# Moving a gating branch's input products between two stages of a two-block transformer kernel

## The chip, the cores and the metric

One core of a Trainium2 chip runs the whole kernel. The metric is the device time of one execution in microseconds, median of three runs. PE is TensorE (the matrix engine), DVE is VectorE, ACT is ScalarE, POOL is GpSimd, SP is SyncE, which here issues nearly all DMAs.

## What is computed

The reference has two blocks on 1024 tokens of width 1024. The first (two attention-like mixers) ends with y @ w_out and a layer norm. The second is the one that most of the change is in:

```python
mod = c @ ada_w[l] + ada_b[l]
shift1, scale1, gate1, shift2, scale2, gate2 = jnp.split(mod, 6, axis=-1)
h = _modulate(_rmsnorm(x, norm1_g[l]), shift1, scale1)
z = h @ w_in[l]
zu, zv, zr = jnp.split(z, [GMLP_WIDTH, 2 * GMLP_WIDTH], axis=-1)
y_a = _gmlp_mixer(zu, zv, ...)      # u = gelu(zu); v = layer_norm(gelu(zv)); u * (causal mix of v)
y_b = _rwkv7_mixer(zr, ...)         # r, k, v and low-rank xw, xa, xg; decay from tanh(xw) @ w2,
                                    # a from xa @ a2, gate from sigmoid(xg) @ g2; scan over tokens
y = jnp.concatenate([y_a, y_b], axis=-1) @ w_out[l]
x = x + gate1[:, None, :] * y
h = _modulate(_rmsnorm(x, norm2_g[l]), shift2, scale2)
y = _hier_moe(h, ...)
```

GMLP_WIDTH is 512, so zu and zv are 1024 columns of w_in; the RWKV part is 512 wide, 8 heads of 64, with low-rank widths 32 (xw), 32 (xa) and 96 (xg). All arithmetic named here is fp32. A 128x128 by 128x512 product in fp32 shows in the trace as two matmul instructions with a weight load each.

## The kernel before, in words

The kernel is a chain of stages with a barrier between them; in a stage each engine has its own instruction list, ordered by hand and tied by semaphores. PSUM's eight banks form two rings of four: ring A is emptied by ACT, ring D by DVE. A `take` of a bank waits until its use four takes ago is freed. Each engine does its list strictly in order.

**stage_out** (line 629, run for both layers of the first block) multiplies the 12 chunks of yT by w_out (six DMAs of 1 MB, `wo_landed`). For each of 8 token tiles it runs hf 0 over all 12 chunks, then hf 1 (L674); DVE adds the residual and normalises while PE is at the next tile; PE then turns the tile before (L615 for the second layer).

**stage_rwkv_pairs** (line 1399, 1669 to 2239 us) works on pairs of heads, c = 0 to 3, by a `script` that PE, ACT and DVE all follow. First `lora`: three groups of low-rank columns (32, 32 and 96 wide) against hT (L1494), 16 products each. Then the front of pair 0: `proj` r, k, v (L1504, weights in three buffers), `small` (L1515), `sums` (L1524, whose result feeds DVE's longest chain, with a reciprocal over 128x1024). Then per pair:

- `turn`: transposes of v, k, b, a (L1536) and the bonus (L1541);
- `A`: five products ab, X, ak, rb, rk (L1552), two ring D banks each; DVE masks ab (L1918, 1921, 1922) and X (L1924, L1925) before the others, and ak and rb need the banks of ab and X;
- `AV` (L1582), then five `level`s (L1562, L1569, L1573). After each level of pair c stands one step of the front of pair c + 1: proj r, k, v, small, sums. For the last pair there is none;
- `tail`: GH (L1593, four ring A banks, emptied by ACT, L1821), then MT (L1603), N (L1611, L1612), Q (L1619) on ring D (DVE, L1944 to L1951), then Yi (L1626, L1627) on ring A (ACT, L1824). SP stores MT, N, Q and Yi to DRAM (L1663, L1664).

ACT does the square roots and exponentials of `sums` (c + 1) (L1778 to L1783) before the GH copies of `tail` (c), since that is the script's order; DVE likewise does its `sums` before MT.

**stage_mix** (line 1976, 2239 to 2580 us) goes over token tiles t in a software pipeline. One iteration of PE is: u(t) (L2044), chain(2t) (L2059), v(t), chain(2t + 1), mix(t-1) (L2067), the RWKV rows(t-1) (L2079) with the gate product g (L2084), turn(t-2) (L2092), out(t-3) (L2100), the norm's turn(t-4) (L615), router(t-5) (L2108). The chain carries the state T from half tile to half tile: PE multiplies by mt, DVE adds n and scales (`step`, L2280, L2282), and the next chain product needs that. DVE's iteration is step(2t), gmlp_norm(t) (L2286 to L2295), step(2t + 1), gmlp_rows(t-1) (L2301, L2303), rwkv_rows(t-1) (L2311 to L2327), normalise(t-4), residual(t-3) (L2337, L2339). ACT's is gelu of u (L2229) and of v (L2232), square roots, copies of yT, and the norm's evacuation (L624). Weights for u and v (w_uv, 4 MB in two DMAs, L2145 and L2152) and the streams mt, n, qt, yi, v (256 KB each and tile) come on SP's queue, as do w_o (4 MB) and a store of zeros (7.7 MB) to the slots of the experts' stage.

## Time and profile before

| | us |
|---|---|
| median of 3 runs | 3325.42 (3325.37 to 3328.36) |
| the profiled execution | 3325.81 |
| its span in the profile | 3324.0 |
| PE busy | 2963.1 (89%) |
| DVE busy | 1724.7 (52%) |
| ACT busy | 1074.7 (32%) |
| POOL busy | 382.3 (12%) |

How to read what follows. Times are microseconds from the start of the span. Engines: PE is matmuls, PEld weight loads beside them. PEclk is the clock granted to TensorE as a share of 2.4 GHz; it has two levels, 1.0 and 0.5. A row of a timeline gives start, length, engine, line, operation, output <- inputs and how many instructions are merged in it (xN); in square brackets stands the idle time of that engine just before and what ended it. Matmuls are pipelined: each record is longer than the distance to the next.

### The profile page before, as it was taken

The numbers are of one execution on the slowest core, as the hardware profiler recorded it, in microseconds if no ns is written. First come the engines' busy times: TensorE is split into PE (matmuls) and PEld (weight loads), VectorE is DVE, ScalarE is ACT, GpSimd is POOL, SyncE is SP. The second block draws the span as 40 slices with busy tenths as digits, with TensorE's granted clock in tenths as the row PEclk, the third lists the DMA queues.
The fourth block names the chain that finished last, engine by engine and source line by source line (L and its number), as shares of the span: only waits on it lengthen the run. The fifth ranks groups of instructions, "written<-read, shape, count | busy, mean of one in ns | idle before, by whom it ended". The sixth has DMA issues, their size and how long they took to land. (4 is left out here: it accounts for less than half of the span.)

```text
span 3324.0 us, 44902 instructions
## 1 busy us (share of the span) xinstructions
PE 2963.1 (89%) x18196; PEld 2026.1 (61%) x18196; DVE 1724.7 (52%) x2719; ACT 1074.7 (32%) x1660; POOL 382.3 (12%) x318
## 2 busy tenths in 40 slices
PE   7999799898699999979987898877999499999990
PEld 6877544545577777754435666674555377777770
DVE  2223323454366665643316435533444699999984
ACT  2111100121355454441122212211223256565652
POOL 1322000000222222200021011010000000000001
PEclk9999899998899999989998897988999699999995
DMA  4111021741211121121011011028222699999985
GB/s 149 48 42 42 36 103 45 218 157 51 76 51 58 53 69 57 52 99 56 36 35 27 10 44 53 2 72 283 64 70 76 214 391 398 399 397 399 397 317 221
DMA packets 282433, 445.87 MB, mean 134 GB/s; under 512 B 14944, under 2 KB 148576, under 8 KB 282256
## 3 DMA queue, kind: packets, MB, share of 16 engines
q1 hardware_dynamic: 275200, 417.66, 35.7%
q0 software_dynamic: 7056, 25.69, 2.0%
q8 instruction: 130, 2.13, 0.3%
q14 instruction: 47, 0.39, 0.0%
HBM read 385.58 MB, written 57.74 MB: 133 GB/s over the span
## 5 line engine op out<-in xcount | busy, mean ns | idle before, releaser
L674 PE MATMUL psum<-wo,yT 128*128 128x512 f32 x768 | 337.7, 599 | 18.8 <-DMA wo<-in_w_out 18.7
L674 PEld LDWEIGHTS psum<-wo,yT 128*128 128x128 f32 x768 | 145.7, 192 | 201.4 <-issue 174.8
L906 PE MATMUL psum<-x_hi,w_hi 128*128 128x512 f32 x512 | 211.4, 413 | 29.4 <-POOL w_lo L1007 28.7
L1096 DVE TENSOR_TENSOR fox_pT_lo<-psum,fox_pT_hi 128x512 fp32r<-128x512 f32 (+2 forms) x192 | 107.1, 558 | 183.6 <-ACT fox_pT_hi L1035 174.4
L908 PE MATMUL psum<-x_hi,w_lo 128*128 128x512 f32 x512 | 201.5, 394 | 0.0
L907 PE MATMUL psum<-x_lo,w_hi 128*128 128x512 f32 x512 | 200.6, 392 | 0.0
L1504 PE MATMUL psum<-hT,wr 128*128 128x512 f32 x384 | 168.5, 597 | 0.0
L2699 ACT CAST hi_d<-land_d 128x2048 fp32r<-128x2048 f32 x66 | 122.7, 1908 | 140.5 <-PE psum L2571 140.5
L162 PE MATMUL psum<-x_hi,w_hi 128*128 128x512 f32 x384 | 151.9, 396 | 8.8 <-POOL w_lo L153 8.8
L2844 DVE TENSOR_TENSOR lo_d<-land_d,hi_d 128x2048 fp32r<-128x2048 f32 x66 | 148.3, 2288 | 21.5 <-ACT hi_d L2699 21.5
L1005 POOL CAST w_hi<-w_land 128x1024 fp32r<-128x1024 f32 x48 | 49.8, 1037 | 911.2 <-DMA w_land<-in_w_in 515.7
L163 PE MATMUL psum<-x_lo,w_hi 128*128 128x512 f32 x384 | 151.2, 394 | 0.0
L164 PE MATMUL psum<-x_hi,w_lo 128*128 128x512 f32 x384 | 150.7, 392 | 0.0
L2844 DVE TENSOR_TENSOR lo_g<-land_g,hi_g 128x2048 fp32r<-128x2048 f32 x66 | 150.6, 2283 | 0.0
L735 DVE SCALAR_TENSOR_TENSOR x_tile<-x_tile,psum 128x512 f32<-128x512 f32 x32 | 22.0, 688 | 244.0 <-PE psum L674 198.0
L1046 ACT ACTIVATE fox_p<-fox_p,fox_bias 128x256 f32<-128x256 f32 (+7 forms) x128 | 99.6, 778 | 120.2 <-DVE fox_bias L1082 116.3
L1504 PEld LDWEIGHTS psum<-hT,wr 128*128 128x128 f32 x384 | 72.8, 191 | 89.3 <-issue 88.7
L906 PEld LDWEIGHTS psum<-x_hi,w_hi 128*128 128x128 f32 x512 | 96.9, 189 | 48.3 <-POOL w_lo L1007 30.1
L2699 ACT CAST hi_g<-land_g 128x2048 fp32r<-128x2048 f32 x66 | 125.2, 1898 | 0.9 <-DMA land_g<-in_moe_w_gate 0.8
L2044 PE MATMUL psum<-w_uv,hT 128*128 128x512 f32 x256 | 117.0, 612 | 7.7 <-DMA rb<-in_router_expert_b 7.7
L2569 PE MATMUL psum<-hi_d,e_h_hi 128*128 128x512 f32 x264 | 116.5, 441 | 6.7 <-DVE e_h_lo L2861 6.7
L1079 DVE CUSTOM_DVE_ANT_0 fox_p<-psum,ncum 128x256 f32<-128x256 f32 (+7 forms) x128 | 97.0, 758 | 48.8 <-PE psum L925 40.2
(478 smaller groups left out, 6345.1 us busy)
## 6 DMA issues: line engine op xcount, KB each, us to landing
land_g<-in_moe_w_gate SPq DMA_DIRECT2D x66, 1024.0 KB, 8.0
land_u<-in_moe_w_up SPq DMA_DIRECT2D x66, 1024.0 KB, 9.1
land_d<-in_moe_w_down SPq DMA_DIRECT2D x66, 1024.0 KB, 9.6
ada<-in_ada_w SPq DMA_DIRECT2D x24, 1024.0 KB, 5.3
y_slots<-yb SPq DMA_DIRECT2D x33, 512.0 KB, 10.4
w<-in_w_in SPq DMA_DIRECT2D x24, 512.0 KB, 3.8
wo<-in_w_out SPq DMA_DIRECT2D x12, 1024.0 KB, 10.7
w_land<-in_w_in SPq DMA_DIRECT2D x24, 512.0 KB, 3.8
```

What stands on the lines that cost most here:

```text
L162: self.nc.tensor.matmul(bank[:], hi[:, d, :], E.x_hi[:, d, cols], start=(d == 0), stop=False)
L163: self.nc.tensor.matmul(bank[:], hi[:, d, :], E.x_lo[:, d, cols], start=False, stop=False)
L164: last = self.nc.tensor.matmul(bank[:], lo[:, d, :], E.x_hi[:, d, cols], start=False, stop=(d == ND - 1))
L674: last = nc.tensor.matmul(bank[:], E.yT[:, c, t * P:(t + 1) * P], wo[:, c, hf * HALF:(hf + 1) * HALF], start=(c == 0), stop=(c == NY - 1))
L906: nc.tensor.matmul(bank[:], hi[:, d, :], E.x_hi[:, d, cols], start=(d == 0), stop=False)
L907: nc.tensor.matmul(bank[:], hi[:, d, :], E.x_lo[:, d, cols], start=False, stop=False)
L908: last = nc.tensor.matmul(bank[:], lo[:, d, :], E.x_hi[:, d, cols], start=False, stop=(d == ND - 1))
L1504: last = nc.tensor.matmul(bank[:], w[m % NW][:, d, :], E.hT[:, d, hf * HALF:(hf + 1) * HALF], start=(d == 0), stop=(d == ND - 1))
L2044: last = nc.tensor.matmul(bank[:], E.hT[:, d, t * P:(t + 1) * P], w_uv[:, d, i * GW:(i + 1) * GW], start=(d == 0), stop=(d == ND - 1))
L2569: nc.tensor.matmul(bank, hi_t, hi_w, start=start, stop=False)
L2699: nc.scalar.copy(w_hi[x][:], land[x][:]).then_inc(hi_set[x], 1)
L2844: V.tensor_tensor(w_lo[x][:], land[x][:], w_hi[x][:].bitcast(F32), ALU.subtract).then_inc(lo_set[x], 1)
```

## The change

Five things change, and only these:

1. The 16 products for u and v of stage_mix (8 x 512 columns and 8 x 512) leave it. They are made in stage_rwkv_pairs as 32 units `("uv", q, t)`: for q = 0 to 3, a quarter (256) of the 1024 columns, and token tile t. A unit is 8 products, 16 instructions, of 256 columns on a ring A bank. `fill` says where they stand in the script: one after `small`(0), three before turn(0), one after X, ak, GH and N of each pair, one after levels 3 and 4 of pairs 1 to 3, one after rk and level 2 of pairs 1 and 2, two after Yi of pair 3. ACT copies each into one of two row buffers, SP stores it (128 KB) to `uv_dram`. `w_uv` now holds one quarter (1 MB); SP loads the next one when the last unit of a quarter is done.
2. stage_mix reads u and v as a stream of 512 KB tiles; gelu takes it from there. hT is freed before the stage, and w_uv is no longer loaded in it.
3. The low-rank groups xw and xa become one group of 64 columns (`xwa`), with w2 and a2 stacked in one tensor.
4. SP loads the projection weights for pair c + 1 one at a time in the script's order, where before it loaded three after the turn.
5. stage_out goes by chunk: for each chunk c both halves, with two banks taken first. (The line of w_o in stage_mix is only written differently: it was and is an fp32 product.)

The diff, cut to its core:

```diff
+                    banks = []
                     for hf in range(2):
                         bank, free = ringD.take(("y", t, hf))
                         wait(pe, ringD.free, free)
-                        for c in range(NY):
-                            if t == 0 and hf == 0 and c % 2 == 0:
-                                pe.wait_ge(wo_landed[c // 2], 16)
-                            last = nc.tensor.matmul(bank[:], E.yT[:, c, t * P:(t + 1) * P], wo[:, c, hf * HALF:(hf + 1) * HALF],
+                        banks.append(bank)
+                    for c in range(NY):
+                        if t == 0 and c % 2 == 0:
+                            pe.wait_ge(wo_landed[c // 2], 16)
+                        for hf in range(2):
+                            last = nc.tensor.matmul(banks[hf][:], E.yT[:, c, t * P:(t + 1) * P], wo[:, c, hf * HALF:(hf + 1) * HALF],
                                                     start=(c == 0), stop=(c == NY - 1))
-                        last.then_inc(ringD.full, 1)
+                            if c == NY - 1:
+                                last.then_inc(ringD.full, 1)
...
+        LORAS = ((0, 2 * LORA), (2 * LORA, GATE_LORA))
+        mu_x = [E.sb(f"mu_x{i}", [n, 1], ctx=st) for i, (_, n) in enumerate(LORAS)]
+        xwa = E.sb("xwa", [2 * LORA, S], ctx=st)
+        of_w, of_a = slice(0, LORA), slice(LORA, 2 * LORA)
...
+        w_uv = E.sb("w_uv", [P, ND, UVW], ctx=st)
+        uv_rows = [E.sb(f"uv_rows{i}", [P, UVW], ctx=st) for i in range(2)]
+        uv_landed, uv_stored = E.sem("w_uv_landed"), [E.sem(f"uv_stored{i}") for i in range(2)]
...
+        w_in = A["w_in_2"][0].rearrange("(c p) n -> p c n", p=P)
+        win = w_in[:, :, 2 * GW:]
...
+        fill = {("small", 0): 1, ("first", 0): 3}
+        for c in range(NPAIR):
+            fill |= {("X", c): 1, ("ak", c): 1, ("GH", c): 1, ("N", c): 1}
+            if c > 0:
+                fill |= {("level", c, 3): 1, ("level", c, 4): 1}
+                fill |= {("Yi", c): 2} if c == NPAIR - 1 else {("rk", c): 1, ("level", c, 2): 1}
+        units = [(q, t) for q in range(2 * GW // UVW) for t in range(NT)]
+        assert sum(fill.values()) == len(units)
...
-        script += [(f[0], 0, *f[1:]) for f in first_front]
+        for f in first_front:
+            script.append((f[0], 0, *f[1:]))
+            if f[0] == "small":
+                script.append(("fill", "small", 0))
+        script.append(("fill", "first", 0))
         for c in range(NPAIR):
             script.append(("turn", c))
             script.append(("A", c))
             script.append(("AV", c))
             for m in range(1, LEVELS + 1):
                 script.append(("level", c, m))
+                script.append(("fill", "level", c, m))
                 if c + 1 < NPAIR:
                     f = front[m - 1]
                     script.append((f[0], c + 1, *f[1:]))
...
-                    for i, (lo, n) in enumerate(((0, LORA), (LORA, LORA), (2 * LORA, GATE_LORA))):
+                    for i, (lo, n) in enumerate(LORAS):
...
-                    for name, m, x in (("w", w2, xw), ("a", a2, xa)):
+                    for name, rows in (("w", of_w), ("a", of_a)):
                         for hf in range(NH):
                             bank = take(ringA, (name, c, hf))
-                            nc.tensor.matmul(bank[:], m[:, c * P:(c + 1) * P], x[:, hf * HALF:(hf + 1) * HALF],
+                            nc.tensor.matmul(bank[:], wa2[rows, c * P:(c + 1) * P], xwa[rows, hf * HALF:(hf + 1) * HALF],
                                              start=True, stop=True).then_inc(ringA.full, 1)
...
+                turns = iter(units)
+
+                def fill_(*at_):
+                    for _ in range(fill.get(at_, 0)):
+                        q, t = next(turns)
+                        if t == 0:
+                            pe.wait_ge(uv_landed, 16 * (q + 1))
+                        bank = take(ringA, ("uv", q, t))
+                        for d in range(ND):
+                            last = nc.tensor.matmul(bank[:, 0:UVW], E.hT[:, d, t * P:(t + 1) * P], w_uv[:, d, :],
+                                                    start=(d == 0), stop=(d == ND - 1))
+                        last.then_inc(ringA.full, 1)
...
+                        fill_(name, c)
...
+                def load_uv(q):
+                    if q > 0:
+                        sp.wait_ge(ringA.full, ringA.nth(("uv", q - 1, NT - 1)))
+                    sp.dma_start(w_uv[:], w_in[:, :, q * UVW:(q + 1) * UVW]).then_inc(uv_landed, 16)
+
+                def fill_(*at_):
+                    for _ in range(fill.get(at_, 0)):
+                        q, t = next(turns)
+                        if t == NT - 1 and q + 1 < 2 * GW // UVW:
+                            load_uv(q + 1)
+                        n = q * NT + t
+                        sp.wait_ge(ringA.free, ringA.nth(("uv", q, t)))
+                        sp.dma_start(E.uv_dram[:, t, q * UVW:(q + 1) * UVW], uv_rows[n % 2][:]).then_inc(uv_stored[n % 2], 16)
+
+                def proj(c, kind):
+                    m = 3 * c + KIND.index(kind) + NW
+                    if m < 3 * NPAIR:
+                        load(m)
+
+                def turn(c):
                     sp.wait_ge(ringA.free, ringA.nth(("tv", c, 1)))
                     sp.dma_start(E.v_dram[:, :, c * P:(c + 1) * P], tok["v"][:]).then_inc(S_["rstore"], 16)
-                    for m in range(NW + 3 * c, min(NW + 3 * c + 3, 3 * NPAIR)):
-                        load(m)
+
+                def a_part(c):
+                    for name in ("ab", "X", "ak", "rb", "rk"):
+                        fill_(name, c)
+
+                def tail(c):
+                    fill_("GH", c)
+                    fill_("N", c)
                     sp.wait_ge(ringD.free, ringD.nth(("Q", c, 1)))
                     sp.wait_ge(ringA.free, ringA.nth(("Yi", c, 1)))
                     for to, src in ((E.mt_dram, MTs), (E.n_dram, Ns), (E.qt_dram, QTs)):
                         sp.dma_start(to[:, c * S:(c + 1) * S], src).then_inc(S_["stored"], 16)
                     sp.dma_start(E.yi_dram[:, :, c * P:(c + 1) * P], Yi).then_inc(S_["stored"], 16)
+                    fill_("Yi", c)
...
+                def fill_(*at_):
+                    for _ in range(fill.get(at_, 0)):
+                        q, t = next(turns)
+                        n = q * NT + t
+                        bank = got(("uv", q, t))
+                        if n >= 2:
+                            act.wait_ge(uv_stored[n % 2], 16 * (n // 2))
+                        nc.scalar.copy(uv_rows[n % 2][:], bank[:, 0:UVW]).then_inc(ringA.free, 1)
...
-                def uv(t, i):
-                    bank = take(ringA, ("u" if i == 0 else "v", t))
-                    for d in range(ND):
-                        last = nc.tensor.matmul(bank[:], E.hT[:, d, t * P:(t + 1) * P], w_uv[:, d, i * GW:(i + 1) * GW],
-                                                start=(d == 0), stop=(d == ND - 1))
-                    last.then_inc(ringA.full, 1)
...
-                        if t == 0:
-                            pe.wait_ge(w_landed["u"], 16)
-                        uv(t, 0)
                         chain(2 * t)
-                        if t == 0:
-                            pe.wait_ge(w_landed["v"], 16)
-                        uv(t, 1)
                         chain(2 * t + 1)
...
                         else:
                             sp.wait_ge(sems["yb"], t - 1)
-                    if x in ("yi", "v"):
-                        src = {"yi": E.yi_dram, "v": E.v_dram}[x][:, t, :]
+                    if x in ("uv", "yi", "v"):
+                        src = {"uv": E.uv_dram, "yi": E.yi_dram, "v": E.v_dram}[x][:, t, :]
                         sp.dma_start(to[:], src).then_inc(landed[x][t % 2], 16)
                     else:
...
+                        act.wait_ge(landed["uv"][t % 2], 16 * (t // 2 + 1))
+                        nc.scalar.activation(u[t % 2][:], stream["uv"][t % 2][:, 0:GW], ACT.Gelu_apprx_tanh)
                         if t >= 1:
                             act.wait_ge(sems["vn"], t)
-                        nc.scalar.activation(vg[:], got(("v", t))[:], ACT.Gelu_apprx_tanh).then_inc(ringA.free, 1)
+                        nc.scalar.activation(vg[:], stream["uv"][t % 2][:, GW:2 * GW], ACT.Gelu_apprx_tanh).then_inc(sems["uv_used"], 1)
                         act.wait_ge(sems["var"], t + 1)
...
-                    dve.wait_ge(ringA.free, ringA.nth(("v", t)))
+                    dve.wait_ge(sems["uv_used"], t + 1)
...
+            modulated.close()
             E.run(stage_mix, A, x2_rows, x3_rows, n3_rows, y_slots)
-        modulated.close()
         with ExitStack() as third:
```

## Rows read from the trace of the kernel before

**Rows 1.** By stretch: length, busy PE, PEld, DVE, ACT, POOL, PEclk, DMA share, GB/s.
```profile
1669.00:2239.00 570.00, 490.76 (x7632) 344.32 (x7632) 250.88 (x266) 125.84 (x197) 82.45 (x104) 0.88 0.11 33
...
2239.00:2307.00 68.00, 45.01 (x186) 22.35 (x186) 17.46 (x35) 12.09 (x16) 1.42 (x2) 0.83 1.01 343
2307.00:2511.00 204.00, 198.76 (x940) 107.80 (x940) 95.07 (x178) 49.62 (x94) 0.00 (x0) 0.97 0.20 66
```

**Rows 2.** Waits of PE, 1669 to 2239: in total, times, longest.
```profile
PE psum L1552 <- DVE Xm L1925: 16.0, 4, 4.6
PE psum L1603 <- ACT GH L1821: 14.9, 4, 4.7
```

**Rows 3.** Timelines of PE, ACT and DVE, RWKV stage, pairs 0, 1 and 3.
```profile
1883.45 2.02 ACT L1821 COPY GH<-psum 128x512 f32<-128x512 f32 x4
...
1885.52 3.00 PE L1603 MATMUL psum<-tok_b,GH 64*64 64x64 f32 x58 [4.73 <-ACT GH L1821]
...
1897.55 1.28 DVE L1944 TENSOR_TENSOR L<-psum,ident 128x512 f32<-128x512 f32 x2
...
1898.29 3.00 PE L1619 MATMUL psum<-rbT,GH 64*64 64x64 f32 x58 [3.23 <-DVE L L1944]
...
1918.54 1.16 PE L1552 MATMUL psum<-at,k 64*64 64x64 f32 x64 [3.17 <-DVE abT L1918]
...
1930.57 2.08 PE L1562 MATMUL psum<-Xm,L 64*64 64x64 f32 x64
...
2218.91 1.73 PE L1603 MATMUL psum<-tok_b,GH 64*64 64x64 f32 x58 [0.68 <-ACT GH L1821]
```

**Rows 4.** Timeline of PE, start of the RWKV stage to the first turn.
```profile
1674.41 42.97 PE L1494 MATMUL psum<-hT,w_lora 128*32 128x512 f32 x96 [8.17 <-DMA w_lora<-in_w_in]
...
1750.33 3.75 PE L1524 MATMUL psum<-tmp,blocksum 128*128 128x512 f32 x4 [1.86 <-issue]
...
1777.42 1.97 PE L1536 MATMUL psum<-ident,v 128*128 128x128 f32 x8 [8.69 <-DVE v L1837]
```

**Rows 5.** Busy time by stretch, tail of pair 0; the clock is third from the end.
```profile
1886.00:1905.00 19.00, 15.77 (x316) 15.58 (x315) 15.09 (x16) 0.00 (x0) 0.00 (x0) 0.50 0.01 2
```

**Rows 6.** Timeline of PE, mixing stage: first out products, then the turn of tile 5.
```profile
2348.33 14.59 PE L2100 MATMUL psum<-w_o,y2T 128*128 128x512 f32 x32
...
2398.02 1.04 PE L615 MATMUL psum<-ident,n_rows 128*128 128x128 f32 x8
2398.89 7.03 PE L2044 MATMUL psum<-w_uv,hT 128*128 128x512 f32 x16
...
2418.58 1.13 PE L2084 MATMUL psum<-g,xg 96*128 96x512 f32 x2 [0.97 <-DVEq L2281]
...
2420.42 13.90 PE L2100 MATMUL psum<-w_o,y2T 128*128 128x512 f32 x32
...
2435.03 1.87 PE L2108 MATMUL psum<-rw,h2T 128*128 128x36 f32 x16
...
2436.73 7.11 PE L2044 MATMUL psum<-w_uv,hT 128*128 128x512 f32 x16
```

**Rows 7.** DMA issues, start of the mixing stage: count, KB each, us to landing.
```profile
y_slots<-zeros SPq DMA_DIRECT2D x1, 7680.0 KB, 37.0
w_uv<-in_w_in SPq DMA_DIRECT2D x2, 2048.0 KB, 9.9
```

**Rows 8.** Timeline of PE, start of the mixing stage.
```profile
2307.22 1.12 PE L2059 MATMUL psum<-T,s_mt 64*64 64x64 f32 x16 [9.09 <-DMA s_mt<-mt]
```

**Rows 9.** Timelines of ACT and DVE, mixing stage, the turn of tile 5.
```profile
2398.66 2.90 ACT L624 ACTIVATE h2T<-psum,mod 128x128 f32<-128x128 f32 x8 [8.06 <-PE psum L615]
2406.01 1.28 ACT L2229 ACT_TABLE_LOAD   x1 [4.45 <-PE psum L2044]
...
2416.13 0.55 DVE L2293 TENSOR_SCALAR vn<-vg,g_mv,g_rstd 128x512 f32<-128x512 f32 x1
```

**Rows 10.** Timeline of PE, first tile of the first output stage.
```profile
424.25 16.15 PE L674 MATMUL psum<-wo,yT 128*128 128x512 f32 x37 [0.57 <-DMA wo<-in_w_out]
```

75 lines of the change are left out of this document (44 added, 31 removed).

## The prediction

> **What bounds the kernel now.** The page's busy times are means over stages with different limits, so I read the table by stretch first, then who waited for whom, then the order of instructions in one pair of heads and in one token tile. Two stages are touched in earnest. The RWKV stage runs from 1669 to 2239 us: 570 us with PE busy 490.8 at a mean clock of 0.88 [rows 1], so 79 us in which PE is idle and more in which it runs at half clock. The mixing stage runs from 2239 to 2580: PE is busy only 45 of its first 68 us, where the DMA engines are full (share 1.01), then 198.8 of 204 us at clock 0.97 [rows 1]. So the mixing stage's middle ends when PE ends, and the RWKV stage has holes. The change moves PE work from the full stage to the one with holes.
>
> The holes of the RWKV stage have five addresses: before the fourth product of the A part (16.0 us over four pairs) and after GH (14.9) [rows 2], before the third A product and before Q (3.2 each, one of four and of three shown [rows 3]), and once before the first turn of v (8.7 [rows 4]). With them go low-clock stretches: the granted clock is 0.50 (1.2 of 2.4 GHz) from 1886 to 1905 [rows 5], after PE had sat idle 4.7 us [rows 3].
>
> **The size of a unit.** In the mixing stage 32 matmul instructions of 512 columns leave at 0.435 us each (13.9 us for 32) [rows 6]. A unit is 16 instructions of 256 columns. No row has that shape in fp32. Lower bound: half of 0.435, 3.5 us a unit; the 128-column transposes at 0.11 us each (8 in 0.87 us from start to start) lie on the same line [rows 6]. Upper bound: the weight load isn't hidden; 16 router instructions of 36 columns, which are little but a load, take 1.7 us from start to start [rows 6], so 3.5 + 1.7 = 5.2. I take 3.5, since at 128 columns, with twice the loads per column, the load is already covered. All 32 units: 111 us, as much as the 16 u and v products that leave (16 x 7.0 = 112).
>
> The Trainium skill ("TensorE: Matmul & The Clock Gate", Part 3: Packing small matmuls) says that a weight load overlaps running matmuls only when it goes to other rows of the array. By that rule the twice as many loads of the units would stand in the open and each unit would cost 5.2 us. The trace disagrees for this kernel: the 0.435 us spacing holds with a load per matmul, and 128-column transposes at 0.11 us keep pace with theirs [rows 6].
>
> **RWKV stage, stretch by stretch** (before: after).
> 1. Start to the first turn: low-rank products 43.0, two projections 27.6, small 3.6, idle 1.9, sums 3.6 at half clock, third projection 14.7, idle 8.7 = 103.1 [rows 4]. After: joining the first two groups removes 32 of 96 instructions, 13.9 us: 29.1 left; 27.6; 3.6; one unit 3.5; sums 1.8 at full clock; 13.9; three units 10.4 = 89.9. DVE's chain to v hangs on sums, and sums starts at the same distance as before (the unit takes 1.6 more than the idle time, sums ends 1.8 sooner), so v is ready as PE gets there. **-13.2.**
> 2. First pair from turn to level 1: 24.6. After: transposes at full clock 3.5, bonus 1.8, first two A products 2.0; then DVE's chain from them to Xm takes 8.7 us whatever PE does, and two units with the third product (8.0) fit in it; then 2.0 and AV 1.9 = 19.9. **-4.7.**
> 3. The same stretch from the end of X on, in pairs 1 to 3: 15.3, 15.0, 13.1 (pair 1, from 1915.4 to level 1 at 1930.6, is in [rows 3]). After: DVE 9.0, products 2.0, a third unit 3.5 that nothing covers, AV 1.9 = 16.4 twice; in the last pair, without the third unit, 11.9. **+1.3.**
> 4. Levels. Eight units stand between levels: three each in pairs 1 and 2, two in pair 3. In pairs 1 and 2 a projection already fills that place; in pair 3, where no projection is left, level still follows level without idle time. All in the open: 27.8, less half of the 3.2 us that pair 1 loses to a low clock there. **+26.2.**
> 5. Tails 0 to 2, from the end of GH to the next turn: 27.1. The unit after GH doesn't start at once: its bank is the one of the first GH quarter, which ACT frees only when it has done the next pair's square roots and exponentials (its GH copies run 1883.45 to 1885.5 [rows 3]). So 3.3 us of the 4.7 stay idle and the unit ends 2.0 us after the old start of MT. That costs nothing: MT's banks are emptied by DVE at 1898.2, because DVE first does the next pair's sums, whatever PE does [rows 3]. After that Q and Yi take 6.3 at full clock (as in the last pair) for 9.6 now: -3.3 at best. At half clock all through, unit 7, MT and N 9.4, unit 7, Q and Yi 9.6 give +9; if only the first unit is slow, +2 at most. I take -2.5, nearer the good end, as a unit is the dense work after which the clock comes back. **-7.5.**
> 6. Last tail to the first DMA of the mixing stage: idle 0.7 [rows 3], MT and N 5.2, Q and Yi 6.3, stores and barrier 8.8 = 21.0. After: four units in the open (13.9) + 5.2 + 6.3, and 5.4 for the copy, store and barrier (the large stores now run under the last units) = 30.8. **+9.8.**
>
> Sum: **+11.9**, bounds +8 and +27. What comes with the units: ACT's copy of 256 columns, at most the 0.5 us of a GH copy's 512 columns [rows 3], in places where ACT waits anyway. A 128 KB store on SP's queue, where it stands before nothing that PE waits for within 7 us. A 1 MB load of the next quarter's columns, queued when a quarter's last product is done: under the 9.9 us that 2 MB of the same matrix take [rows 7], while Q, Yi and the turn give at least 13. Without that cover both together would cost up to 10 us at three places. The projection weights are now loaded one by one a pair ahead: later in SP's order, but still 100 us before use.
>
> **Mixing stage.** *Start.* PE reaches the first chain product of tile 2 at 2307.2, after 9.1 us of waiting for s_mt [rows 8], queued behind 4 MB of w_uv, 4 MB of w_o and 7.7 MB of zeros [rows 7]. 4 MB less at about 390 GB/s is 10.3 us, three uv tiles of 0.5 MB give back 3.8: **-6.5**. Bounds: -3 (tiles 0 and 1 on DVE, some 30 us from 2264 on at the latest, don't bind even then) and -10.3.
>
> *A turn.* One token tile now costs PE 37.8 us, 14.0 of them u and v [rows 6]. Without these 23.8 of PE's work are left, but a loop appears that u and v covered: the turn of the norm on PE, ACT's eight activations (2.9), table load and first gelu (1.9), second gelu 0.6, DVE's statistics 0.9, ACT's root 0.4, DVE's normalise and the first operation of the chain step (2.5), and only then does the bank for g come free [rows 9]. From the start of a turn ACT is free at 1.0, the second gelu ends at 3.5, DVE's normalise starts at 5.4, g can start at 7.85; PE arrives at 5.95: of the 19.7 us to g in [rows 6] 4.7 are left without u, v and the wait, and 1.3 come new between the two chain products, for DVE's step. So PE waits 1.9 there, and a full turn is 7.85 + g 1.0 + turn 0.9 + out 13.7 + norm 0.9 + router 1.7 = 26.0 for 37.8. DVE is busy 95.1 us of 204 and ACT 49.6 [rows 1], 17.6 and 9.2 a turn, so neither is full at 26. The turns in order, saved: tile 2 9; tile 3 13.9 (no norm yet: PE's 5.95 decides); tile 4 13.7; tile 5 10.1 (norm just before, no router to cover ACT); tile 6 11.8; tile 7 11.8, where out waits for the bank of mix = **-70.3**. The drain after 2511 has no u and v and stays.
>
> *Clock.* Each turn now has 3 us of waits among short products. Before, with the 1.0 us before g, the first turn with out products still ran them in 14.6 instead of 13.9 [rows 6]. I charge two of six turns with 4 us: **+8** (bounds 0 and 27).
>
> **Out products by chunk** in both output stages. PE waits 0.6 for a chunk of w_out four times at most, since a chunk brings it 1.7 us of work and takes 2.55 to land; with both halves it brings 3.4. The first tile ends at 436.2 now and 411.4 + 20.5 + 3.4 of low clock = 435.3 after [rows 10], but the last tile's first half is finished late, +0.6. **-0.5** for each stage, -1 in all (0 to -2). The mixing stage's w_o line is only rewritten; "stay fp32" is no edit of this diff and costs nothing.
>
> **Sum** against the profiled execution (3325.8 us, span 3324.0): +11.9 - 6.5 - 70.3 + 8 - 1 = -57.9. The median of the runs is 3325.4, so the forecast is **3267.5 us**.
>
> **Rivals.** (a) *The clock stays low.* The 3.3 us left after GH and the waits in the turns drop it each time: tails +2.3 for -2.5 (+14), all six turns (+16): 3298. For it: the drop of [rows 5] followed such an idle time. Against: units follow. 0.20. (b) *The loop doesn't bind.* ACT and DVE run ahead and the turns go at PE's own work, with no clock loss: about 25 less, 3242. Against it stands the 0.97 us that g waits already in each turn [rows 6]. 0.08. (c) *Weight loads in the open*: 512 loads at the router's 0.106 us are 54 us, some 4 of it in holes: 3318. 0.03; against it the two spacings of [rows 6]. (This is the Trainium skill's rule above.) (d) *The other side: turns are held by something other than PE*, the x tile (two buffers, stored before reloaded) or the streams on SP's queue, which I have at 24.5 us into a turn. The RWKV stage then pays (+12 to +27) and the turns give nothing back: with +25, 3343. It decides once a turn shortens by less than 1.8 us; that DVE is busy under half of a turn [rows 1] speaks against it. 0.06, a third of it within 0.2%.
>
> **How the numbers follow.** Forecast case (3253 to 3283) 0.63, (a) 0.20, (b) 0.08, (c) 0.03, (d) 0.06. The range 3246 to 3298 leaves out (c), (d), half of (b) and under half of (a). Faster by over 0.2% (6.6 us, about what can be told from no change): 0.92; same 0.04; slower 0.04.
>
> **What would show it.** Units of 3.5 us in the fill places; no wait before Q longer than 3 us and none before the third A product; a unit after GH that starts on ACT's copy; the RWKV stage near 582 us; turns of 26 us with g waiting about 2 on DVE; s_mt of tile 2 about 61 us after the mixing stage's first DMA. Units of 5 us, turns above 30 or clock near 0.8 in the turns would make it wrong.

## The result, and the profile after

The changed kernel takes 3276.6 us (median of 4 runs, 3275.64 to 3278.82), the kernel before 3326.89 beside it: ratio 0.9848, 95% interval 0.9831 to 0.9865. The profiled execution took 3275.64 (span 3273.9), 50.2 less than the one of before. Forecast were 57.9 less.

Where the 50 us come from, by the first and last instructions of each stretch in the two profiles (the mixing stage is measured from its first DMA to the last turn of the norm, the row that waits 3.25 us for n_rows):

| stretch | before | after | difference | forecast |
|---|---|---|---|---|
| up to the RWKV stage's first DMA | 1669.63 | 1664.91 | -4.7 | -1.0 |
| RWKV stage | 569.56 | 582.95 | +13.4 | +11.9 |
| mixing stage: start, to the chain of tile 2 | 68.03 | 61.93 | -6.1 | -6.5 |
| mixing stage: the six turns of tiles 2 to 7 | | | -51.2 | -62.3 |
| the rest | | | -1.5 | 0 |

The first row is mostly not the change's. Of the 4.7 us 3.9 arise between 600 and 860 us, which the diff doesn't touch, and over the thirteen profiled kernels of this study the start of the RWKV stage lies anywhere from 1662.1 to 1669.6, whether the output stages run by chunk or not. So below I compare lengths of the two stages, which repeat: the RWKV stage of the unchanged script is 569.6, 571.3 and 571.3 in three profiles, that of the changed one 582.3 to 583.2 in five; the mixing stage of before is 330.2 to 330.6 in three.

Busy time by stretch, after the change (length, then busy PE, PEld, DVE, ACT, POOL, granted clock of PE, DMA share, GB/s); it answers to [rows 1]:

```profile
1665.00:2248.00 583.00, 555.34 (x8112) 404.86 (x8112) 247.85 (x264) 134.74 (x227) 82.71 (x105) 0.98 0.15 46
2248.00:2310.00 62.00, 13.65 (x110) 10.98 (x112) 17.56 (x35) 11.06 (x15) 1.28 (x2) 0.50 1.02 341
2310.00:2462.00 152.00, 135.53 (x760) 86.98 (x758) 95.52 (x178) 49.88 (x94) 0.00 (x0) 0.85 0.31 102
```

The RWKV stage has 27.7 us of idle PE for 79, at a clock of 0.98 for 0.88. The mixing stage's middle, which ran at 0.97 with PE full, is now at 0.85 with 16 us idle. Its start is 62 us long with 13.65 of PE work in it.

The start of the RWKV stage, timeline of PE (start, length, engine, line, what, count, idle time before in brackets), for [rows 4]:

```profile
1669.52 30.16 PE L1516 MATMUL psum<-hT,w_lora 128*64 128x512 f32 x64 [7.98 <-DMA w_lora<-in_w_in]
...
1727.07 1.99 PE L1537 MATMUL psum<-xwa,wa 32*128 32x512 f32 x8
1729.06 3.69 PE L1575 MATMUL psum<-w_uv,hT 128*128 128x256 f32 x16
1732.59 1.88 PE L1546 MATMUL psum<-tmp,blocksum 128*128 128x512 f32 x4
1734.30 13.90 PE L1526 MATMUL psum<-hT,wr 128*128 128x512 f32 x32
1748.04 10.52 PE L1575 MATMUL psum<-w_uv,hT 128*128 128x256 f32 x48
1758.40 1.04 PE L1558 MATMUL psum<-ident,v 128*128 128x128 f32 x8
```

No row but the first waits. A unit's 16 products leave in 3.5 us (1732.59 - 1729.06), and 48 in 10.4. First turn 93.5 us after the first DMA, 107.8 before: -14.3 for -13.2.

The tail of pair 0, same view, for [rows 3]:

```profile
1861.84 5.41 PE L1575 MATMUL psum<-w_uv,hT 128*128 128x256 f32 x16 [3.27 <-ACT GH L1908]
1867.17 1.74 PE L1640 MATMUL psum<-tok_b,GH 64*64 64x64 f32 x58
...
1872.49 3.72 PE L1575 MATMUL psum<-w_uv,hT 128*128 128x256 f32 x16
1876.15 1.73 PE L1657 MATMUL psum<-rbT,GH 64*64 64x64 f32 x58
...
1882.59 1.09 PE L1558 MATMUL psum<-ident,v 128*128 128x128 f32 x8
```

The unit waits for its bank, runs slowly itself (5.41), and MT, N, Q and the next turn run at the full clock: 1.7 for 3.0 us, and no wait before Q.

The mixing stage, PE, its start and the turns of tiles 2 and 3, for [rows 6] and [rows 8]:

```profile
2309.79 1.12 PE L2143 MATMUL psum<-T,s_mt 64*64 64x64 f32 x16 [28.12 <-DMA s_mt<-mt]
2312.11 1.12 PE L2143 MATMUL psum<-T,s_mt 64*64 64x64 f32 x16 [1.20 <-DVE T L2361]
2313.15 3.67 PE L2151 MATMUL psum<-vn,wsT 128*128 128x64 f32 x16
2316.76 2.58 PE L2163 MATMUL psum<-T,s_qt 64*64 64x64 f32 x32
2319.26 2.07 PE L2168 MATMUL psum<-g,xg 96*128 96x512 f32 x2
2321.13 1.82 PE L2176 MATMUL psum<-ident,y 128*128 128x128 f32 x8
2322.88 0.68 PE L2143 MATMUL psum<-T,s_mt 64*64 64x64 f32 x16
2328.59 1.12 PE L2143 MATMUL psum<-T,s_mt 64*64 64x64 f32 x16 [5.03 <-DVE T L2361]
2329.64 3.67 PE L2151 MATMUL psum<-vn,wsT 128*128 128x64 f32 x16
2333.24 2.58 PE L2163 MATMUL psum<-T,s_qt 64*64 64x64 f32 x32
...
2339.32 14.13 PE L2185 MATMUL psum<-w_o,y2T 128*128 128x512 f32 x32
```

Two things are new here. PE waits 28.12 us for s_mt, since the u and v products that stood there are gone while the zeros' 37.6 us store still lies ahead of it. And chain(7) waits 5.03 us for DVE. The products between stand at the half clock (mix 3.67 for 2.00 us, rows 2.58 for 1.54, g 2.07 for 1.12, turn 1.82 for 1.04).

The six turns, from one even chain product to the next (the last one ends with the mix product behind it), took 13.1, 30.5, 28.0, 29.3, 27.6 and 24.4 us. Before they took 18.6, 37.0, 36.1, 37.8, 37.9 and 36.5; there a turn begins with u(t), ahead of the chain product, and only that of tile 2 is counted from the chain product. The granted clock by turn, after the change, was 0.51, 0.77, 0.82, 0.94, 0.88 and 1.00.

### The profile page after: what moved, and what is told of

It reads as the page before. It is cut to its first block and busy times, and to the rows that moved or that the text cites. A ratio compares the mean times of both kernels' runs of the same rounds, so it can differ in the third digit from the quotient of the medians.

```text
span 3273.9 us, 45458 instructions
## 1 busy us (share of the span) xinstructions
PE 2932.8 (90%) x18420; PEld 2057.4 (63%) x18420; DVE 1722.8 (53%) x2717; ACT 1083.2 (33%) x1690; POOL 383.0 (12%) x318
## 3 DMA queue, kind: packets, MB, share of 16 engines
HBM read 389.77 MB, written 61.93 MB: 138 GB/s over the span
## 5 line engine op out<-in xcount | busy, mean ns | idle before, releaser
L910 PE MATMUL psum<-x_hi,w_hi 128*128 128x512 f32 x512 | 212.0, 414 | 29.1 <-POOL w_lo L1011 28.4
L1575 PE MATMUL psum<-w_uv,hT 128*128 128x256 f32 x512 | 124.3, 399 | 9.8 <-ACT GH L1908 9.8
```

The lines of the kernel that those rows point to most:

```text
L910: nc.tensor.matmul(bank[:], hi[:, d, :], E.x_hi[:, d, cols], start=(d == 0), stop=False)
L1575: last = nc.tensor.matmul(bank[:, 0:UVW], E.hT[:, d, t * P:(t + 1) * P], w_uv[:, d, :], start=(d == 0), stop=(d == ND - 1))
```

## Experiments

All stage lengths are from the profiled executions; "mix" is measured as in the table above. The expectations below measure it to the first DMA of the next stage, which gives 340.6 before and 283.3 after the change for the 330.5 and 273.2 here. Each ratio is to runs of before on the same chip, whose medians were 3320.97 to 3326.89.

| kernel | RWKV stage | mix | median us | ratio to before |
|---|---|---|---|---|
| before | 569.56 | 330.49 | 3325.42 | 1 |
| after | 582.95 | 273.22 | 3276.6 | 0.9848 (0.9831 to 0.9865) |
| e1_join | 550.73 | 330.16 | 3300.01 | 0.9935 (0.9919 to 0.9952) |
| e2_chunk | 571.33 | 330.58 | 3320.19 | 0.9993 (0.9983 to 1.0003) |
| e3_units_eighth | 560.58 | 271.72 | 3251.5 | single run |
| e4_warm_start | 582.32 | 273.05 | 3275.7 | 0.9858 (0.9841 to 0.9874) |
| e5_warm_turns | 582.92 | 265.50 | 3267.6 | 0.9831 (0.9814 to 0.9847) |
| e6_zeros_late | 583.23 | 252.78 | 3255.24 | 0.9789 (0.9773 to 0.9805) |
| e7_before_zeros_late | 571.32 | 323.35 | 3311.77 | 0.9957 (0.9943 to 0.9971) |
| e8_late_warm | 582.46 | 240.33 | 3243.66 | 0.9760 (0.9741 to 0.9778) |
| e9_units_double | 687.94 | 274.00 | 3381.84 | single run |
| e10_two_groups | 596.56 | 273.10 | 3288.76 | single run |
| e11_interleaved | 588.71 | 273.23 | 3278.49 | single run |

### One part of the change alone: join, and chunk order

e1_join is the kernel before with the joined tiles of the diff; its core:

```diff
+        LORAS = ((0, 2 * LORA), (2 * LORA, GATE_LORA))
...
-                    for i, (lo, n) in enumerate(((0, LORA), (LORA, LORA), (2 * LORA, GATE_LORA))):
+                    for i, (lo, n) in enumerate(LORAS):
...
-                            nc.tensor.matmul(bank[:], m[:, c * P:(c + 1) * P], x[:, hf * HALF:(hf + 1) * HALF],
+                            nc.tensor.matmul(bank[:], wa2[rows, c * P:(c + 1) * P], xwa[rows, hf * HALF:(hf + 1) * HALF],
```

> The kernel before with one part of the change alone: the w and a low-rank columns are joined (64 weight-load/product groups for 96, tiles wa2 and xwa), nothing else. Ledger of the prediction: the low-rank products fall from 43.0 to about 28.7 us, the sums and their wait shrink, so the RWKV stage (from its first DMA to the mix stage's first DMA) comes out 13.2 us shorter than before's 569.6, near 556.4; the small products on w and a side by side (8 in 1.99 us after the change, against 4 and 4 in 3.6 before) could take up to 2 more, so 554.5 to 556.5. The mix stage stays at 340.6. Total about -13 to -15 us, 0.995 to 0.996 of before. Rival, the start of the stage does not bind (the first pair waits for something that does not move, a load or VectorE): less than 5 us, 0.999.

Measured: RWKV stage 550.73, 18.8 us less than before's, 20.6 less than in the two other profiles of the unchanged script; ratio 0.9935. More than expected. By pair, from the first DMA to the store of MT of pairs 0, 1, 2 and 3: 223.4, 127.4, 126.6, 65.3 for 239.1, 130.6, 127.0, 64.8. PE at the start:

```profile
1671.12 29.96 PE L1494 MATMUL psum<-hT,w_lora 128*64 128x512 f32 x64 [8.20 <-DMA w_lora<-in_w_in]
...
1728.47 1.99 PE L1515 MATMUL psum<-xwa,wa 32*128 32x512 f32 x8
1733.47 3.63 PE L1524 MATMUL psum<-tmp,blocksum 128*128 128x512 f32 x4 [3.00 <-ACT tmp L1771]
...
1760.42 1.97 PE L1536 MATMUL psum<-ident,v 128*128 128x128 f32 x8 [9.59 <-DVE v L1837]
```

Of the 43.0 us 13.0 are gone, and the small products take 1.99 for 3.7 (they lie in rows 0 to 31 and 32 to 63 now), which turns up as a longer wait for ACT: the first turn comes 94.1 us after the first DMA for 107.8, -13.7. That is the forecast's term. The other 5 us lie behind, 2.0 in pair 0 and 3.2 in pair 1, where the products are the same, at a clock of 0.88 for 0.86 in both. 4.0 of them lie in the levels: from level 1 to the end of GH pairs 0, 1 and 2 take 78.2 us each here, where each of the three profiles of the unchanged script has one pair at 81.4 or 81.5 and the others at 78.8 to 80.3. What puts those pairs there isn't shown.

e2_chunk is the kernel before with the order of the out products changed:

```diff
-                        for c in range(NY):
...
+                    for c in range(NY):
...
+                        for hf in range(2):
```

> The kernel before with one part of the change alone: the out products of the mix stage are ordered by chunk, both halves for a chunk, where before had one half after the other. Ledger of the prediction: a gain of about 1 us in all, from the first tile's loads of wo, none from the turns; mix stage 339 to 341 (before 340.6), total 0 to -2 us. Rival 1: sharing each chunk's weights between two products saves weight loads, about 16 x 0.06 us a tile, some 8 us over 8 tiles. Rival 2: holding two banks at once makes out wait for the copies of the tile before it: 1 to 2 us a turn slower, +8 to +16.

The expectation names the wrong stage: the edit is that of the two output stages of the first block, as in the diff, and the mixing stage's out products stay. Its numbers can be held against those stages. From the first DMA of one to that of the next stage, the first took 188.8 us before, 188.8 in e1, 188.1 here and 188.5 after the change; the second 194.2, 194.1, 193.1 and 192.9. So -0.3 to -0.7 and -1.1 to -1.3; the ratio of the runs is 0.9993, interval 0.9983 to 1.0003, not to be told from nothing. All the profiles together do tell it: the two stages take 188.8 and 194.3 us on average in the three kernels with the old order and 187.3 and 193.0 in the ten with the new one, and in each stage every one of the ten lies below every one of the three. That is -1.5 and -1.3 for the ledger's -0.5 each. Both rivals of the expectation, 8 us less and 8 to 16 more, are out.

### What the units cost, and what paid for them

e3 leaves out seven of the eight products of each unit in the changed kernel:

```diff
-                        for d in range(ND):
-                            last = nc.tensor.matmul(bank[:, 0:UVW], E.hT[:, d, t * P:(t + 1) * P], w_uv[:, d, :],
-                                                    start=(d == 0), stop=(d == ND - 1))
+                        last = nc.tensor.matmul(bank[:, 0:UVW], E.hT[:, 0, t * P:(t + 1) * P], w_uv[:, 0, :], start=True, stop=True)
```

> The changed kernel with each of the 32 units cut to its first of eight products (the u/v products over seven of the eight chunks of h are left out; copies, banks, waits and all other work stay). 32 units then cost 32 x 0.44 = 14 us of TensorE time where they cost 32 x 3.5 = 112, so 98 us of work leaves the RWKV stage. Ledger: about 14 of the 32 units (8 in the levels, 2 beside the products of r and k, 4 at the end) lay in the open, and the others in time in which TensorE waited anyway; the stage falls by 14 x 3.05 = 43 us less what a lower clock gives back, so by 30 to 43 from 583.0. Rival, every unit in the open (nothing of the waits was filled): -98. Rival, units only fill waits: 0 to -10. The mix stage stays at 283 within 2.

Measured: 560.58, 22.4 less than 583.0. Below the 30 to 43 of the ledger, and neither rival. The stretch as a whole:

```profile
1664.00:2225.00 561.00, 489.07 (x7664) 346.16 (x7664) 248.24 (x264) 134.63 (x227) 82.88 (x105) 0.90 0.16 48
```

Beside the first row of after this gives a balance. The units' products are busy 26.7 us here for 124.3, 97.6 less. PE's busy time fell by 66.3 only, its idle time rose by 44.3 (71.9 for 27.7), the stretch is 22.0 shorter. So of 97.6 us of unit work 44 fill idle time, 31 come back, since the other products are busy that much less, at a granted clock of 0.98 for 0.90, and 22 lengthen the stage. The waits that came back are the addresses of [rows 2] and [rows 4]: in this run PE waits 12.4 us for Xm, 10.1 for abT, 8.3 for v and 6.3 before Q.

e9 does the reverse, each unit's products twice:

```diff
-                        for d in range(ND):
+                        for d in tuple(range(ND)) * 2:
```

> The changed kernel with the eight products of each of the 32 units issued twice (the second pass overwrites the first), 32 x 3.5 = 112 us more for TensorE in the RWKV stage. In the run with eighths of units the first 98 us of unit work made this stage only 22.4 longer: 44 went into idle time and 31 came back through the clock (0.88 to 0.98). If holes and clock are what paid for it, they are used up now: idle time of TensorE is 28 us, most of it at the stage's start, end and ahead of the unit after GH, where a unit can't go, and the clock is 0.98. The second set then costs 95 to 112: stage 678 to 695 from 583. Rival, units run cheaply because products of this shape overlap other work on TensorE: the second set costs as little as the first, +30 to +50.

Measured: 687.94, +105.0 for 112 us more of products. The group of the units (busy, mean ns of one, idle time ahead):

```profile
L1575 PE MATMUL psum<-w_uv,hT 128*128 128x256 f32 x1024 | 230.3, 384 | 9.8 <-ACT GH L1908 9.8
```

Seven eighths of the first set cost 0.23 us of stage for each us of work, the second set 0.94. So the units aren't cheap in themselves: holes and clock paid, and both are used up (PE is idle 27.5 us of 688 at a clock of 0.99). The 9.8 us of wait after GH (the same in all three kernels) is the one hole that a unit at that place can't fill, as it waits for it itself.

### The turns: clock or VectorE?

e4 puts products into the 28 us wait at the start of the mixing stage:

```diff
+                LONG = {4: 30}
+                def warm(bank, n):
+                    for _ in range(n):
+                        nc.tensor.matmul(bank[:], E.ident[:], wsT[:, 0:4, :].rearrange("p h n -> p (h n)"), start=True, stop=True)
...
+                    if c in LONG:
+                        early = take(ringD, ("T", c))
+                        warm(early, LONG[c])
```

> The changed kernel with 30 extra 128x512 fp32 products (about 26 us at the low clock, 13 at the full) on TensorE just ahead of its wait for s_mt of tile 2, in a bank whose content the chain then overwrites; they lie in the 28.12 us in which TensorE waits there. If the half clock after that wait is what turns 2 to 4 lost against the forecast: the granted clock of 2309:2410 rises from 0.69..0.94 to near 1.00, turn 2 falls from 13.1 by about 4, turn 3 by 2 to 4, turn 4 by 0 to 1, total -5 to -9 us (0.997 to 0.998 of after). If the waits on VectorE and ScalarE bind in these turns and the clock is only their sign: the clock rises and the time stays within 2 us. If the products outlast the wait: slower by up to 5.

Measured: mix 273.05, 0.2 less than after; the time is the same. Timeline of PE:

```profile
2310.83 0.68 PE L2153 MATMUL psum<-T,s_mt 64*64 64x64 f32 x16
2312.70 0.68 PE L2153 MATMUL psum<-T,s_mt 64*64 64x64 f32 x16 [1.20 <-DVE T L2371]
2313.32 2.00 PE L2161 MATMUL psum<-vn,wsT 128*128 128x64 f32 x16
2315.24 1.54 PE L2173 MATMUL psum<-T,s_qt 64*64 64x64 f32 x32
...
2318.65 0.68 PE L2153 MATMUL psum<-T,s_mt 64*64 64x64 f32 x16
2327.95 1.12 PE L2153 MATMUL psum<-T,s_mt 64*64 64x64 f32 x16 [8.62 <-DVE T L2371]
2329.00 3.67 PE L2161 MATMUL psum<-vn,wsT 128*128 128x64 f32 x16
```

The clock did rise, and turn 2 shrank from 13.1 to 7.8 us. But chain(7) now waits 8.62 for 5.03, and what follows is slow again. Chain(7) comes 78.9 us after the stage's first DMA for 80.7: of 5.3 us at the full clock DVE lets 1.9 through. The next two turns give these back, since there the out products, 15.16 and 15.33 us for 14.13 and 14.35, run longer at the half clock. What DVE does last until chain(7), in the changed kernel:

```profile
2326.61 0.69 DVE L2406 TENSOR_TENSOR y<-y,psum 128x512 f32<-128x512 f32 x1
2327.54 0.42 DVE L2359 TENSOR_TENSOR T<-psum,s_n 128x256 f32<-128x256 f32 x1 [0.24 <-DVE y L2406]
2328.11 0.42 DVE L2361 TENSOR_TENSOR T<-T,carry 128x256 f32<-128x256 f32 x1
```

DVE's list has rwkv_rows(t-1) ahead of step(2t + 2), so one iteration of DVE without residual and norm, some 16.5 us (2311.06 to 2327.54; 15.2 in e4, where its waits for PE inside are shorter), stands between the first step of tile 2 and chain(7), whatever PE does, since there are no out products to cover it.

e5 therefore fills that wait too, and the ones behind it (LONG by chain product, GLONG by tile ahead of g):

```diff
+                LONG, GLONG = {4: 30, 7: 9, 9: 2, 11: 1, 13: 1}, {4: 4}
...
+                        warm(early_yT[0], GLONG.get(t, 1))
```

> The changed kernel with extra fp32 products of 512 columns on TensorE (0.44 us each at the full clock, in pairs) in the waits of the mix stage: 30 ahead of the chain of tile 2 as in the run before, 9 ahead of chain(7), which waited 8.6 us for VectorE there, 2, 1 and 1 ahead of the next odd chains, and 1 (4 for tile 4) ahead of each g product. The run before showed that the full clock of turn 2 alone buys nothing, since chain(7) waits for VectorE's rwkv_rows until 18 us after the start either way. If the half clock of turns 3 to 6 is what the forecast lacked (mix 3.67 for 2.00, rows 2.57 for 1.54, g 2.07 for 1.12, turn 1.91 for 1.04, so 4.6 a turn): granted clock near 1.00 from 2310 on, turns 3 to 5 shorter by 3 to 4.6 each, turn 6 by 2, less 0.9 a turn for the products where nothing waits: total -6 to -12 us against the changed kernel (0.996 to 0.998 of it). If VectorE binds these turns too, its waits (1.99, 3.37, 0.55) grow by what the products lose, and the total stays within 2 us. If the clock does not follow such products: no change of the clock and +5.

Measured: mix 265.50, -7.7. Turns of tiles 2 to 6: 13.4, 29.1, 24.1, 27.6, 25.9 for 13.1, 30.5, 28.0, 29.3, 27.6.

```profile
2324.15 7.99 PE L2137 MATMUL psum<-wsT,ident 128*128 128x512 f32 x18
2332.07 0.68 PE L2154 MATMUL psum<-T,s_mt 64*64 64x64 f32 x16
2332.68 2.00 PE L2162 MATMUL psum<-vn,wsT 128*128 128x64 f32 x16
2334.61 1.54 PE L2174 MATMUL psum<-T,s_qt 64*64 64x64 f32 x32
2336.08 1.13 PE L2137 MATMUL psum<-wsT,ident 128*128 128x512 f32 x2
2337.04 1.02 PE L2183 MATMUL psum<-g,xg 96*128 96x512 f32 x2
...
2338.78 13.90 PE L2200 MATMUL psum<-w_o,y2T 128*128 128x512 f32 x32
```

The granted clock is 1.00 from 2323 to 2455 (0.61 from 2310 to 2323: it fell again after the chain of tile 2, which in e4 it didn't). Work that computes nothing makes the stage shorter. So the half clock of turns 3 to 6 did cost time: at least 7.7 us, more by what the extra products took where nothing waited. In turn 3 the nine products overshot by 4.2 us: DVE's T was written at 2327.83, and chain(7) ran at 2332.07.

### The start: what the move uncovered

The zeros' store is cut into five and issued at SP's iterations 3 to 7 of the mixing stage, in the changed kernel (e6) and in the one before (e7):

```diff
-                sp.dma_start(further, zeros[:].rearrange("p (o n) -> p o n", o=1).broadcast_to([P, OVER * D // ZW, ZW])).then_inc(zeroed, 16)
+                PART = OVER * D // ZW // 5
+
+                def zero(i):
+                    sp.dma_start(further[:, i * PART:(i + 1) * PART, :], zeros[:].rearrange("p (o n) -> p o n", o=1).broadcast_to([P, PART, ZW])).then_inc(zeroed, 16)
...
+                    if 3 <= t < 8:
+                        zero(t - 3)
```

> The changed kernel with the store of zeros (7680 KB, 37 us of the DMA queues) cut into five parts that are issued behind the loads of tiles 4 to 8 instead of ahead of those of tile 2. If the zeros are what TensorE waits for at the chain of tile 2 (28.12 us): s_mt of tile 2 then stands behind the 4 MB of w_o only, and the chain runs at about 2286 instead of 2309.8, where VectorE's rows of tile 0 end (2287.6); the mix stage falls from 283.3 by 20 to 25, less up to 5 where a part of the zeros makes a later tile's loads late: total -16 to -25 us against the changed kernel (0.992 to 0.995). Rival, something else holds the start (w_o, the loads of tiles 0 and 1 or VectorE): less than 5.

> The kernel before with the same five late parts of zeros. Its chain of tile 2 waited 9.09 us for s_mt, since the input products of the gating branch lay in front; so the same edit should bring 9 us here (7 to 10; 0.997 to 0.998 of before), against 20 to 25 in the changed kernel. The difference of the two is what the move of the input products uncovered at the start and left unused. If both gain alike, the zeros hold something else than this chain.

Measured: e6 mix 252.78, -20.4 against after, ratio 0.9789 to before; e7 mix 323.35, -7.1 against before, ratio 0.9957. PE in e6, and then the same chain product in e7:

```profile
2290.89 1.12 PE L2143 MATMUL psum<-T,s_mt 64*64 64x64 f32 x16 [6.37 <-DMA s_mt<-mt]
...
2309.67 1.12 PE L2143 MATMUL psum<-T,s_mt 64*64 64x64 f32 x16 [4.54 <-DVE T L2366]
```

```profile
2295.80 0.68 PE L2059 MATMUL psum<-T,s_mt 64*64 64x64 f32 x16
```

In e6 the chain of tile 2 comes 40.5 us after the stage's first DMA for 61.9, in e7 58.5 for 68.0 and without a wait. The 13 us between the two gains are what the change laid bare at the start and didn't use: the u and v products had been covering the store of zeros. e7's medians are 14.8 us apart and its profile only 8.9 from that of before: -7.1 in mix, -3.6 ahead of the RWKV stage, the part that varies anyway, and +1.8 in the RWKV stage. The rest isn't in the profile.

e8 has both edits, e6's as it is, and fewer extra products than e5 at the start:

```diff
+                LONG, GLONG = {4: 7, 7: 8, 9: 2, 11: 1, 13: 1}, {4: 3}
```

> The changed kernel with both edits that showed a gain alone: the zeros in five late parts (-21 us alone), and the extra fp32 products in the waits of the mix stage (-9 us alone; here 7 ahead of the chain of tile 2, whose wait is 6.4 us now, 8 ahead of chain(7), 2, 1 and 1 ahead of the next odd chains, 1 ahead of each g, 3 for tile 4). If the two are apart (one takes away a wait for DMA, the other a low clock behind waits for VectorE), they add up: about -30 against the changed kernel, 3245 to 3248, 0.976 of before. If the parts of zeros and the faster turns collide (a turn of 23 us instead of 27 asks for the loads sooner), -21 to -25.

Measured: 3243.66 us, ratio 0.9760 (0.9741 to 0.9778), mix 240.33, so -32.9 where the two alone give -20.4 and -7.7. They add up, and a little more: the turn of tile 2 keeps the full clock too. Tile 3, from chain(6) to chain(8):

```profile
2300.41 0.68 PE L2154 MATMUL psum<-T,s_mt 64*64 64x64 f32 x16
2301.03 7.13 PE L2137 MATMUL psum<-wsT,ident 128*128 128x512 f32 x16
2308.62 0.68 PE L2154 MATMUL psum<-T,s_mt 64*64 64x64 f32 x16 [0.46 <-DVE T L2381]
...
2329.16 0.68 PE L2154 MATMUL psum<-T,s_mt 64*64 64x64 f32 x16
```

The turns are 8.7, 28.8, 24.1, 27.6, 25.9 and 24.4 us, 139.3 in all. e6 is the same kernel without the extra products, and its turns are 13.2, 31.0, 28.0, 29.7, 27.5 and 24.4, in all 153.7, like the 152.7 of after. So in the turns the full clock is worth 14.4 us, extra products included, and 12.5 in the stage; e5, with its overshoot, shows less. In tile 3 the eight products end before DVE does, so there DVE decides. The row from the turn of tile 4 to 15 us past that of tile 7:

```profile
2330.00:2446.00 116.00, 113.34 (x637) 66.45 (x637) 77.65 (x146) 40.12 (x83) 0.00 (x0) 1.00 0.50 166
```

The DMA share is 0.50 with the zeros in it (0.28 over the same work of after), and PE waits for no DMA there. This is the fastest of the kernels here.

### Was the join needed?

e10 keeps the joined tiles and issues the w and a products as two groups for partitions 0 to 31 and 32 to 63 of one bank; e11 has them in turn, with the two loops exchanged. e10's edit:

```diff
-                            for d in range(ND):
-                                last = nc.tensor.matmul(bank[0:n, :], wl[:, d, lo:lo + n], E.hT[:, d, hf * HALF:(hf + 1) * HALF],
+                            for at in (0, LORA) if i == 0 else (0,):
+                                m = LORA if i == 0 else n
+                                for d in range(ND):
+                                    last = nc.tensor.matmul(bank[at:at + m, :], wl[:, d, lo + at:lo + at + m], E.hT[:, d, hf * HALF:(hf + 1) * HALF],
```

> The changed kernel with the joined low-rank products issued as two groups again (w into partitions 0 to 31 of the bank, a into 32 to 63; 96 instructions for 64); the joined tiles and everything behind them stay joined. Ledger: 32 x 0.435 = 13.9 us more on TensorE at the start of the RWKV stage, where nothing covers them: low-rank 44.1 instead of 30.2, stage 583 + 13.9 = 597. Rival, the -18.9 that the join alone gave in the kernel before came mostly from what stands behind it (the small products side by side, the clock): less than 10. Rival, the two groups go to different columns of the array and run side by side: 0.

> The same 96 low-rank products as in the run with two groups, but w and a in turn for each chunk of h, so that each product for partitions 0 to 31 is followed by one for partitions 32 to 63. The run with two groups took 38.7 us for 96 products where 96 at 0.435 would take 42 and the joined 64 took 30.2: 8.5 for 32 more. If products for different column groups of the array overlap where they are neighbours, nearly all 32 pairs do so now: 30 to 32 us for the 96, and the stage 583 to 589. If the 8.5 came from something else (a better clock at the stage's start: the joined group's first products ran at 0.50), 38 to 42 again and the stage near 596. The two-group run also had 5 us of idle time put down to issue in the first two pairs; if that belongs to the changed order it comes again, if it is chance it is gone.

Measured, first products of the RWKV stage in e10, then in e11:

```profile
1668.87 38.66 PE L1518 MATMUL psum<-hT,w_lora 128*32 128x512 f32 x96 [8.02 <-DMA w_lora<-in_w_in]
```

```profile
1666.92 29.50 PE L1518 MATMUL psum<-hT,w_lora 128*32 128x512 f32 x96 [8.22 <-DMA w_lora<-in_w_in]
```

In turn, 96 instructions take as long as 64: each pair of neighbours for different output partitions runs side by side. The Trainium skill ("TensorE: Matmul & The Clock Gate", Part 3: Packing small matmuls) says that products with under 128 rows or columns can run at the same time in different tiles of the array; this trace agrees, and shows besides what order does. A product is two instructions, so in e10 sixteen for one group stand ahead of sixteen for the other. By the starts of the single instructions, four pairs there start within 0.03 us of each other at each of the three changes of group, and all others stand 0.43 us apart at the full clock: 12 pairs, and 38.66 us. In e11 all 32 pairs start together; in before, where both groups go to partitions 0 to 31, none does. So the 13 us of the join in these products were to be had with two groups too, if they go to different output partitions and in turn. The stage of e10 at 596.56 met the expected 597, but by other terms than the expectation named: 8.5 us in the low-rank products, and 5.1 behind. Of these a part is idle time put down to issue, 8.1 us in the stage for 3.8 in after; it came again in e11 (9.2), so it isn't chance. Nor is it the length of the list alone, since e9, with 512 instructions more, has 4.9; why it comes isn't shown. Joined, the stage is 5.8 us shorter than e11's.

## Why the prediction came out as it did

The profiles differ by 50.2 us for the 57.9 forecast, a miss of 7.7. Some of that closeness is luck: the output stages (-1.6), the RWKV stage (+13.4), the start (-6.1) and the turns (-51.2) together give -45.5, which is 12.4 from the forecast, and the other 4.7 come from stretches that the change doesn't touch.

- **The size of a unit: right.** 3.5 us from start to start, rival (c) out: 48 instructions in 10.36 us, 0.216 each with a weight load each. The rule of the Trainium skill that the prediction quotes does not show in these products.
- **RWKV stage: right, step by step.** Against the kernel before, the six steps of the ledger measure -14.3, -3.3, +3.6, +25.2, -6.4 and +8.5 us for -13.2, -4.7, +1.3, +26.2, -7.5 and +9.8. None is off by more than 2.3, and the worst, step 3, has a slip in it: by its own terms the last pair comes to 12.9 and not 11.9, which makes the step +2.3. So the sum, +13.4 for +11.9 (+12.2 against the mean of the three unchanged profiles), doesn't owe its closeness to errors that cancel.
- **The parts, one by one: not as the ledger books them.** Steps 2 to 6 are +32.2 against e1 for +25.1. e1 gains 4.0 us in the levels and 1.5 in the stretch from the first turn to level 1, at a clock of 0.88 for 0.86, and the units, which raise the clock to 0.98, can't gain the same time again. The join alone is worth more than its term, and the units added to it cost more than theirs.
- **The unit after GH: right** in its place and wait (3.27), bank freed by ACT, MT and N at the full clock. The tails come out 3.1, 1.2 and 2.1 us shorter for 2.5 each: the unit itself takes 5.4, 6.7 and 5.2 us, at granted clocks of 0.68, 0.54 and 0.70. The clock of the whole stage, 0.98 for 0.88, has no term of its own in the sum; it is in the steps, which take the products behind a unit at the full clock, and e3 prices it at 31 us of work.
- **Start of the mixing stage: right**, chain of tile 2 at 61.9 us for 61.5, after 28 us of waiting, of which e6 puts 21 down to the zeros. The forecast priced the start by what the DMAs do; that 20 us lay there for the taking it didn't say.
- **The turns: mis-sized, -51.2 for -62.3, the one large miss.** By turn they fell short of the -70.3 by 3.5, 7.4, 5.5, 1.5, 1.5 and -0.3, in all 19.1, of which 8 had been charged as clock. Two terms make up the 11.1. *The clock*, charged for two of six turns: mix, rows, g, turn and out of tiles 3 to 6 run 4.8, 4.9, 1.8 and 2.9 us longer than at the full clock, and e8, which is at the full clock throughout, has turns 13.4 us shorter than after, for 8 charged. *DVE in tile 3*: even in e8 the turns are 5.7 us longer than the forecast has them without its clock term: tile 3 takes 28.8 for 23.1, and the others differ by 0.2 to 1.6 and cancel. The forecast had PE's own work decide there, but DVE's iteration does: chain(7) waits for it in after, in e4 and in e8. The bounds of the clock term (0 and 27) held, its value didn't. Rival (a) had a low clock in turns (+16) and tails (+14) together; the turns' part came, the tails' didn't.
- **Signs of being wrong.** The prediction named turns above 30 us and a clock near 0.8 in the turns. Both came for a part: tile 3 took 30.5 us, and the clock of tiles 3 and 4 was 0.77 and 0.82. They point at the two terms above.
- **g waits on DVE: right where the clock is full.** The forecast has 1.9 us in a full turn and 1.7 more in that of tile 5. Measured were 3.37 in tile 5, which ran at the full clock up to g, and 0.55 in tile 6, where PE arrives later at the half clock.
- **Out by chunk:** small, as forecast, but nearer -2.8 than -1 by all thirteen profiles, just beyond its bounds of 0 and -2.

## What to carry to other kernels

Work that moves out of a full stage into one with holes is paid by the holes and by the clock, until both are used up: the first 98 us cost 22, the next 112 cost 105. Where it moves from, ask what it had been covering, a store that nobody needed soon or another engine's list. What it leaves behind are waits, and here the half clock came with the waits among short products (granted clock 0.51 to 0.94 in tiles 2 to 6) and slowed the rest of the turn. So look first at what can be taken out of the way there (order of the DMAs: 20 us here). Leaving some of the moved work in the waits may be the next thing to try: no run here has that, but even products that compute nothing gave 12.5 us.

## What the runs showed of the hardware

- Two fp32 products of 32 output partitions each run side by side when they go to different partitions and stand near each other in the list: 64 such instructions and 32 others took 29.5 us with the two groups in turn, 38.7 with sixteen of one ahead of sixteen of the other, where four pairs start together at each change of group, and 43.0 when both went to partitions 0 to 31.
- Products that contract over 32 rows do so too: 8 instructions of 512 columns in 1.99 us, the four from rows 0 to 31 starting together with the four from rows 32 to 63 behind them in the list, for 3.7 when all lay in rows 0 to 31.
- Products of 256 columns with a weight load each leave every 0.216 us, half of the 0.435 of 512 columns; 16 of them took 3.72 us at the full clock and 6.71 at a granted clock of 0.54.
- The out products, 32 of 512 columns, take 13.9 us at the full clock and 14.1 to 15.3 where they began at half: the clock rises in them, so most of what a low clock costs lies in the short products ahead.
